# x and the memory tokens also handed over transposed, and loaded feature-major

## The reference

```
def rms_norm(x, g):
    xf = x.astype(jnp.float32)
    y = xf * lax.rsqrt(jnp.mean(xf * xf, axis=-1, keepdims=True) + RMS_EPS)
    return (y * g.astype(jnp.float32)).astype(x.dtype)

def hybrid_layer(x, mem, pos, g_mix, w_in, ..., g_mem, w_mkv, ...):   # x, mem: 1 x 256 x 1024
    h = rms_norm(x, g_mix)
    z = h @ w_in                      # columns: q, k, v of two mixers, q of a third, gates
    ...                               # rope on parts of z, attention of the first two mixers
    o_m = memory_attn(q_m * scale, rms_norm(mem, g_mem), w_mkv)   # keys, values = mem_n @ w_mkv
    ...                               # gates, projections, w_o, then the MLP
```

## Time and profile before

| what | value |
|---|---|
| median of three runs | 1580.24 us |
| span of the profiled execution | 1577.1 us |
| what lies around the span (median less span) | 3.1 us |
| PE busy | 1431.2 us, 91% |
| POOL, DVE, ACT busy | 672.7, 574.6, 555.4 us |
| DMA, mean | 251 GB/s |

### The profile page before, as it was taken

How to read it: one execution, slowest core, us unless ns; L and a number is a source line. 1 busy time by engine, 2 the same in 40 slices (tenths; PEclk the granted TensorE clock), 3 DMA queues, 4 the chain that set the end, 5 groups by cost and what they waited for, 6 DMA issues and landing times.

```text
span 1577.1 us, 17825 instructions
## 1 busy us (share of the span) xinstructions
PE 1431.2 (91%) x7537; PEld 1014.0 (64%) x7537; DVE 574.6 (36%) x885; ACT 555.4 (35%) x713; POOL 672.7 (43%) x187
## 2 busy tenths in 40 slices
PE   8999999999999999999999999999996676676667
PEld 6877788877887778887788888978842121121111
DVE  4532423336262242334643786768510010010001
ACT  6356443433535645444344444574310000000001
POOL 5846588755784658776555774010000000000000
PEclk9999999999999999999999999999998788787778
DMA  8534457588553445759826344113999999999997
GB/s 296 187 110 159 146 175 240 180 305 315 172 184 125 148 145 182 226 179 340 318 83 198 112 150 149 33 68 133 409 411 427 429 427 429 427 428 427 428 427 298
DMA packets 115516, 395.38 MB, mean 251 GB/s; under 512 B 5719, under 2 KB 9620, under 8 KB 101996
## 3 DMA queue, kind: packets, MB, share of 16 engines
q1 hardware_dynamic: 113372, 388.70, 66.3%
q0 software_dynamic: 1520, 4.49, 0.8%
q10 hardware_dynamic: 544, 1.05, 0.2%
HBM read 393.16 MB, written 1.05 MB: 250 GB/s over the span
## 4 chain that ended last, share of the span: by engine, by line
PE 76%; DMA 20%; DVE 2%; ACT 1%; issue 1%; SPq 0%; DVEq 0%; ACTq 0%
PE psum L2283 18%; PE psum L2285 18%; PE psum L2284 18%; DMA ring<-in_w_e_down 7%; PE psum L1241 7%; DMA ring<-in_w_e_gate 6%; DMA ring<-in_w_e_up 6%; PE psum L1156 2%; PE psum L2436 1%; PE psum L2463 1%; PE psum L1017 1%; PE psum L2327 1%; PE psum L2512 1%; DMA ring<-in_w_in 1%; PE psum L1094 1%
## 5 line engine op out<-in xcount | busy, mean ns | idle before, releaser
L657 POOL TENSOR_TENSOR ring_lo<-ring,ring_hi 128x2048 fp32r<-128x2048 f32 x118 | 538.0, 4565 | 231.2 <-ACT ring_hi L637 230.8
L2285 PE MATMUL psum<-ring_hi,hT_hi 128*128 128x512 f32 (+2 forms) x912 | 352.6, 387 | 0.0
L637 ACT ACTIVATE ring_hi<-ring 128x2048 fp32r<-128x2048 f32 (+1 forms) x127 | 239.9, 1889 | 318.3 <-DMA ring<-in_w_down 109.0
L2284 PE MATMUL psum<-ring_lo,hT_hi 128*128 128x512 f32 (+2 forms) x912 | 352.0, 386 | 0.0
L2283 PE MATMUL psum<-ring_hi,hT_lo 128*128 128x512 f32 (+2 forms) x880 | 348.1, 396 | 1.3 <-DVE hT_lo L2610 0.4
L1241 PE MATMUL psum<-arena 128*32 128x512 f32 x796 | 144.2, 706 | 63.5 <-DMA arena<-in_w_e_down 23.7
L2285 PEld LDWEIGHTS psum<-ring_hi,hT_hi 128*128 128x128 f32 x912 | 171.2, 188 | 34.7
L2283 PEld LDWEIGHTS psum<-ring_hi,hT_lo 128*128 128x128 f32 x880 | 165.3, 188 | 41.0 <-issue 6.9
L2284 PEld LDWEIGHTS psum<-ring_lo,hT_hi 128*128 128x128 f32 x912 | 171.5, 188 | 31.1
L1241 PE MATMUL psum<-ring,arena 128*32 128x512 f32 x720 | 132.1, 725 | 59.3 <-DMA ring<-in_w_e_gate 23.1
L1241 PEld LDWEIGHTS psum<-arena 128*32 128x32 f32 x796 | 32.4, 127 | 165.3 <-issue 73.2
(11 more groups left out here) (463 smaller groups left out, 1790.2 us busy)
## 6 DMA issues: line engine op xcount, KB each, us to landing
ring<-in_w_in SPq DMA_DIRECT2D x59, 1024.0 KB, 5.2
ring<-in_w_up SPq DMA_DIRECT2D x32, 1024.0 KB, 5.5
ring<-in_w_down SPq DMA_DIRECT2D x32, 1024.0 KB, 5.3
ring<-in_w_e_down SPq DMA_DIRECT2D x16, 2048.0 KB, 19.5
arena<-in_w_e_up SPq DMA_DIRECT2D x14, 2048.0 KB, 21.2
arena<-in_w_e_down SPq DMA_DIRECT2D x12, 2048.0 KB, 22.7
ring<-in_w_e_gate SPq DMA_DIRECT2D x12, 2048.0 KB, 23.5
arena<-in_w_e_gate SPq DMA_DIRECT2D x12, 2048.0 KB, 22.8
```

What stands on the lines that cost most here:

```text
L637: act.activation(slot_hi(u)[:, 0:c, :], slot(u)[:, 0:c, :], ACT.Copy).then_inc(hi_sb, 1)
L657: eng.tensor_tensor(slot_lo(u)[:, 0:c, :], slot(u)[:, 0:c, :], slot_hi(u)[:, 0:c, :].bitcast(F32), ALU.subtract).then_inc(done, 1)
L2284: pe.matmul(dst, hi(k0 + k), w_lo, start=False, stop=False)
L2285: last = pe.matmul(dst, hi(k0 + k), w_hi, start=False, stop=stop and k == nk - 1)
```

## The change

`x` and `mem` are also handed over transposed (`x_t`, `mem_t`, made on the host).

- Layer 0 loads `xT` (in the place of `xn`) from `x_t` in two halves on ACT's queue. ACT and DVE split it from there, and PE's 16 transposes of `x` are gone; `keep_busy` goes from 4 to 12.
- `x` itself is loaded whole by POOL's queue, which now issues four DMAs in place of two: x, mem, mem_t, constants. The constants get a semaphore of their own. ACT's squares of x wait for that `x`.
- `memT` (SBUF) is loaded in layer 0 by POOL's queue and again in layer 1 by SP's, behind unit 3. PE's 16 transposes of the memory are gone in both layers; DVE's 16 operations on the memory read `memT` where they read PSUM.
- ACT's squares of the memory, its mean, root and reciprocal are made in layer 0 alone.

```diff
-            pe.wait_ge(x_in, 16)
-            half_to_features(x, 0)
-            keep_busy(6, 4)
+            keep_busy(6, 12)
             first_unit()
-            pe.wait_ge(rest_in, 16)
-            half_to_features(x, 1)
...
-                if l == 0:
-                    pe.wait_ge(cols_sb, 2)
-                pe.wait_ge(mem_in, 32)
-                to_features(mem_tok)
                 for n in range(2, 5):
                     pe.wait_ge(z_sb, l * 10 + (2, 4, 6)[n - 2])
...
                 z_tile(0)
                 z_tile(1)
+                if l == 0:
+                    dve.wait_ge(mem_in, 32)
+                else:
+                    dve.wait_ge(late_in, 16 * (N_LATE + l))
                 for half in range(2):
-                    dve.wait_ge(turn_full, l * 8 + 3 + half)
                     for k in range(4):
-                        dve.tensor_scalar(memT_hi[:, c, :], flat[2 + half][:, k * T:(k + 1) * T], gain, None, ALU.mult).then_inc(mem_g, 1)
+                        dve.tensor_scalar(memT_hi[:, c, :], memT[:, c, :], gain, None, ALU.mult).then_inc(mem_g, 1)
...
-                        dve.scalar_tensor_tensor(out=memT_lo[:, c, :], in0=flat[2 + half][:, k * T:(k + 1) * T], scalar=gain,
+                        dve.scalar_tensor_tensor(out=memT_lo[:, c, :], in0=memT[:, c, :], scalar=gain,
                                                  in1=memT_hi[:, c, :].bitcast(F32), op0=ALU.mult, op1=ALU.subtract).then_inc(mem_g, 1)
...
+                    act.wait_ge(rows_in, 16)
+                    squares_half(0, sums, x_sq)
+                    squares_half(1, sums, x_sq)
                     high_parts(4, 4)
+                    act.wait_ge(mem_in, 32)
...
+            pool.dma_start(x[:, :, :], w["x"].rearrange("b (t p) d -> p (b t) d", p=P)).then_inc(rows_in, 16)
             pool.dma_start(mem_tok, w["mem"].rearrange("b (t p) d -> p (b t) d", p=P)).then_inc(mem_in, 16)
-            pool.dma_start(consts[:, P:], w["consts"][:, P:]).then_inc(mem_in, 16)
+            pool.dma_start(memT, w["mem_t"].rearrange("(c p) t -> p c t", p=P)).then_inc(mem_in, 16)
+            pool.dma_start(consts[:, P:], w["consts"][:, P:]).then_inc(tables_in, 16)
```

More of the change, by code:

```diff
@@ L286, in build @@
         mem_sq = carve(18688, TT, D)
+        memT = carve(11264, KC, T)
+        x_sq = carve(16384, TT, D)
+        xT = xn[:, :, :].rearrange("p t (c n) -> p (t c) n", n=T)
         kv_mem = carve(14848, TT, 2 * WM)
@@ L324, in build @@
         mem_in = sem("mem_in")
+        tables_in = sem("tables_in")
         sq_a = sem("sq_a")
@@ L2225, in _ @@
                     load(u, src, l * UNITS1 + u + 1)
+                    if l and u == R1 - 1:
+                        sp.dma_start(memT, w["mem_t"].rearrange("(c p) t -> p c t", p=P)).then_inc(late_in, 16)
                     if l == 0 and u == R1 - 1:
@@ L2570, in _, with low_half @@
         def _(dve):
-            def low_half(half, gain, ready):
+            def low_half(half, gain, ready, features=None):
                 for k in range(4):
@@ L2575, in low_half @@
                         dve.wait_ge(turn_a, ready + k + 2)
-                    dve.scalar_tensor_tensor(out=hT_lo[:, 4 * half + k, :], in0=flat[2 + half][:, k * T:(k + 1) * T],
+                    src = flat[2 + half][:, k * T:(k + 1) * T] if features is None else features[:, 4 * half + k, :]
+                    dve.scalar_tensor_tensor(out=hT_lo[:, 4 * half + k, :], in0=src,
                                              scalar=gain[:, 4 * half + k:4 * half + k + 1],
@@ L2642, in _ @@
             low_piece(0)
-            low_half(0, g_feat[:, 0, 0, :], 0)
+            low_half(0, g_feat[:, 0, 0, :], 0, xT)
             for k in range(1, UC):
@@ L2648, in _ @@
             for l in range(DEPTH):
-                low_half(1, g_feat[:, 0, l, :], l * 18 + 4)
+                low_half(1, g_feat[:, 0, l, :], l * 18 + 4, None if l else xT)
                 if l == 0:
@@ L2889, in _, with high_half, squares_half @@
         def _(act):
[L2890 to L2891 removed]
+            def high_half(half, gain, full, features=None):
+                if features is None:
+                    act.wait_ge(turn_full, full)
+                else:
+                    act.wait_ge((x_in, rest_in)[half], 16)
                 for k in range(4):
[L2893 removed]
+                    src = flat[2 + half][:, k * T:(k + 1) * T] if features is None else features[:, 4 * half + k, :]
+                    act.activation(hT_hi[:, 4 * half + k, :], src, ACT.Copy,
                                    scale=gain[:, 4 * half + k:4 * half + k + 1]).then_inc(turn_a, 1)
[L2896 removed]
+            def squares_half(half, into, junk=xn):
                 for t in range(TT):
[L2898 removed]
+                    act.activation(junk[:, t, half * UN:(half + 1) * UN], x[:, t, half * UN:(half + 1) * UN], ACT.Square, accum_out=into[:, t, half:half + 1])\
                        .then_inc(sq_a, 1)
[L2901 to L2903 removed]
+            x_src = w["x_t"].rearrange("(c p) t -> p c t", p=P)
+            act.dma_start(xT[:, 0:4, :], x_src[:, 0:4, :]).then_inc(x_in, 16)
+            act.dma_start(xT[:, 4:8, :], x_src[:, 4:8, :]).then_inc(rest_in, 16)
             act.wait_ge(cleared, 1)
@@ L2944, in _ @@
                            .then_inc(silu_t, 1)
+                else:
+                    squares_half(0, sums)
+                    squares_half(1, sums)
+                cs = slice(0, TT if l else 2 * TT)
                 act.wait_ge(r_v, l * 7 + 2)
-                act.activation(roots, means, ACT.Sqrt).then_inc(sq_a, 1)
+                act.activation(roots[:, cs], means[:, cs], ACT.Sqrt).then_inc(sq_a, 1)
                 high_parts(5 if l == 0 else 4, 14)
@@ L3064 @@
     arrays["consts"] = constants()[1]
+    arrays["x_t"] = np.ascontiguousarray(np.asarray(inputs["x"])[0].T)
+    arrays["mem_t"] = np.ascontiguousarray(np.asarray(inputs["mem"])[0].T)
     nc = bacc.Bacc("TRN2", target_bir_lowering=False, num_devices=1, dynamic_dma_scratch_size=8192)
```

48 lines of the change are left out of this document (22 added, 26 removed).

## The result

| | before | changed |
|---|---|---|
| median, us | 1580.22 (1579.34 to 1580.82, 4 runs) | 1606.99 (1604.78 to 1614.19, 4 runs) |
| ratio to before | | 1.0177 [1.0165, 1.0189] |
| span of the profiled execution | 1577.1 | 1604.8 |

The account below looks back on a forecast made before the run. PE was taken to bound the kernel, three quarters of the chain. 18.6 (layer 0) + 7.0 (layer 1) + 3.6 (clock) = 29 us took the span from 1577.1 to 1606.3, median 1609 us; range 1583 to 1622.

Parts of the forecast that it names:

- The mechanism: DVE operations in SBUF and POOL splits exclude each other; one DVE operation gets through between back-to-back splits.
- the eight with two inputs alone: Memory operations: only eight of sixteen held, costing 1.8 us less in layer 0 and 5.7 less in layer 1.
- The start: Layer 0's start: removed x transposes hidden, 0 us; POOL's first split at 18.6; cost with z tile 0's wait 2.6 us.
- PE loses 0.9 to 1.4 us; I take 1.3: Before unit 2 of layer 0: low_half(1) may have its last operation behind POOL's first split.
- z tile 0: Layer 0, behind unit 3: copied out at 37.7 after late row factors, PE waiting from 34.6.
- The memory in layer 0: DVE's 16 operations held behind back-to-back POOL splits; PE stalls 16.1 us for z tile 2, loss so far 18.6.
- Layer 1: DVE's 16 operations pass in POOL's gaps; z tile 2 out at 460.8, loss 7.0 us, bounds -1.6 and +13.
- The clock: PE at half speed behind two stalls, 1.8 us each, 3.6 in all, bounds 0 and 5.
- The signs: memT_hi, memT_lo means over 1.5 us; PE idle 10-17 us near 60, 3-14 near 455; halved clock; z tile 0 after 35.
- fours: Rival: splits let DVE's operations through four at a time; 1581.2 us, no change; chance 0.08.
- no exclusion: Rival: memory operations not held, memory lands by 27, transposes saved; 1576.8 us, faster; chance 0.05.
- The transfer: Rival: x, mem and memT loads delay layer 0's row factors until 40, +5; 1583.6 us; chance 0.09.

Follow-up runs that it names:

- e6: Kernel before with the memory's part alone: memT loaded and read in SBUF, row factors once, x as before; 1606.76 us, ratio 1.0181.
- e1: Changed kernel, but ACT copies memT into PSUM and DVE's 16 memory operations read it there; 1587.91 us, ratio 1.0055.
- e8: Changed kernel with memT and the constants loaded behind POOL's split of unit 3; 1608.29 us, ratio 1.0177.
- e10: Changed kernel with x's part alone: the memory turned by PE and read from PSUM again; 1588.97 us, ratio 1.006.
- e2: Changed kernel, but ACT copies xT's second half into PSUM and layer 0's low_half(1) reads it there; 1607.98 us, ratio 1.0174.
- e9: Changed kernel with matmuls whose result nobody reads put into PE's three stalls to keep it busy; 1606.73 us, ratio 1.0163.
- e3: Changed kernel with both x's second half and the memory read by DVE from PSUM; 1585.18 us, ratio 1.0034.
- e5: e3 with memT and the constants loaded behind POOL's split of unit 3; 1580.23 us, ratio 1.0004 to the kernel before.
- e4: Kernel before with one edit: the memory's squares, mean, root and reciprocal made in layer 0 only; 1580.59 us, ratio 1.0001.
- e7: e6 with memT copied to PSUM for DVE, and memT and constants loaded behind POOL's split of unit 3; 1579.68 us, ratio 0.9998.

## Why the prediction was right, and where it was off

**The mechanism.** The sign, the size and the place came from the earlier trace rows, one short operation and one long beside a split, and from the choice to take all sixteen operations as open to being held, on the strength of a single `tensor_scalar`. Both hold: in e6 four `tensor_scalar` in a row take a split each, and e1, which moves an input, gives 19 us back. The other case, "the eight with two inputs alone", falls.

**The start** was right in that the transposes of x hid nothing (unit 1's first matmuls stand at 16.57 in place of 16.45) and in POOL's first split (18.59 for 18.6). The term "PE loses 0.9 to 1.4 us; I take 1.3" was mis-sized: it measured 6.8, and 2 for the clock. I had let `low_half(1)` have at most its last operation behind one split; it was the first, with three behind it, and behind two splits. That one operation gets through between two back-to-back splits was no reading of the rows at all: the `tensor_scalar` of the earlier trace rows ended at 30.69 with the third and last of the three splits (30.65), not with the second, as the prediction has it. The rule came true for the `tensor_scalar` of e6; the `scalar_tensor_tensor` of e8 and e10 did not get in.

**z tile 0** was out at 38.98 (37.57 + 1.41) for the forecast 37.7. ACT reached the memory's squares at 31.61, as forecast (31.5), but for a reason that the forecast lacked: it waited up to 29.80 for unit 4's weights, not for the memory. The rest is a wait that the forecast had taken out, with POOL "idle at the new place": POOL split unit 4 there, from 31.79 to 36.37, and the means of 34.09 ended at 36.39. The 2.6 us were not lost as such, because PE was later still. e2 shows them when PE is on time: 4.45.

**The memory in layer 0**: the 16.1 us supposed POOL's splits of units 5 to 9 back to back. That state exists (e6: 15.94), but in the changed kernel POOL had caught up, by my reading during PE's wait at the start, with gaps of 0.7 to 1.6 us in which DVE got operations through, and the stall was 8.15. The errors nearly cancelled: ahead of z tile 2 the loss was 7.1 us with the clock (6.8 + 2 - 1.7) for 2.6, the stall 8.15 for 16.1, and together 17.4 with the clock for 18.6 and 1.8. That the time came within 2 us of the forecast is luck to this extent.

**Layer 1**: the count in the gaps gave 7.0 us, and with the clock 8.8; measured 8.6. Counted from the same place (17.4 us later than there), z tile 2 was forecast out at 478.2; its first two of four operations are out at 477.8.

**The clock**: 1.8 us for each of two stalls; it was three stalls at about 2 us, e9 measures 2.2 for the third.

**The signs**: the halved clock, the place of the stalls and z tile 0 out after 35 us came. The stall of layer 0 (8.15 us for 10 to 17) and the mean of `memT_hi` (1.44 us for over 1.5; `memT_lo` has 2.08) fell short, since 5 operations of 16 were held and not 7 ahead of a free rest.

**The rivals**: "fours" and "no exclusion" are refuted by e1 and e6. The transfer is real, but as a cause that shows only when the port is out of the way (e3 to e5, about 5 us); in the changed kernel it costs nothing that the median shows (e8). The row factors, which the sum gave no price, are worth nothing (e4).

The sum: forecast 29.2, measured 27.7 on the span. The upper end is given twice, as 1619 from the sum of the bounds and as 1622 for the forecast's range; no term stands for the difference.

## What to carry to other kernels

Before an operand is moved from PSUM to SBUF to save work on the bound engine, ask which engine reads it, and which other engine's work that engine then has to wait behind. Here 16 transposes of the memory, worth some 2 us a layer, were paid with 16 operations that each could last as long as a POOL split. A cost that comes of two engines' timing depends on when they meet; it has to be counted against the other engine's gaps, and an edit elsewhere that shifts one of them by 2 us (e9) can cost more than it brings. Loads that are issued early, because there is room, take their share from the loads that somebody waits for; the same loads issued 9 us later left the kernel level with before (e5).

## What the runs showed of the hardware that was not expected

- Between two back-to-back splits of POOL a waiting `tensor_scalar` got in each time (e6: 4.71 us each, as long as a split), while a waiting `scalar_tensor_tensor` with two SBUF inputs was passed over (10.35 us in the changed kernel, 8.92 in e8, 9.47 in e10, each behind two splits). In e6 a `scalar_tensor_tensor` did run where POOL had paused for 0.19 us. The 9.47 us operation of e10 began 0.08 us before the split, by its record. The Trainium skill ("SBUF — State Buffer", section "Who interferes with whom") says that the order of issue decides who is blocked; the start in the record does not tell it here. Why the one kind gets in and the other doesn't stays open; the second was seen in one place of the program only, so the place may matter and not the kind.
- A load of 1 MB on SP's queue took 13.0 us beside 4 MB on POOL's, and 6.7 beside 2 MB in the kernel before.
- The 2 us that e7 gains in the layers aren't to be seen at the end. Whether the DMA-bound experts swallow them or the runs can't tell them is open.
